# The last norm of a two-layer decoder trunk: weights applied early by ScalarE, the factor by VectorE and GpSimd

## What is computed

```python
def rmsnorm(x, g, eps=NORM_EPS):
    x32 = x.astype(jnp.float32)
    y = x32 * lax.rsqrt(jnp.mean(x32 * x32, axis=-1, keepdims=True) + eps)
    return (y * g.astype(jnp.float32)).astype(x.dtype)
...
        x = x + gt2 * conv_gated_mlp(h2, ffn_up[l], ffn_conv_w[l], ffn_conv_b[l], ffn_down[l])
    return rmsnorm(x, final_g)
```

## Time and profile before

| | us |
|---|---|
| median of three runs | 1070.72 |
| range of the three | 1070.26 to 1072.43 |
| the profiled execution, its own time | 1072.69 |
| its span, first to last instruction | 1070.9 |
| PE busy | 1048.0 (98%) |
| DVE busy | 849.9 (79%) |
| ACT busy | 587.2 (55%) |
| POOL busy | 115.6 (11%) |

### The profile page before, as it was taken

One profiled execution on the slowest core, in us unless ns is written; L12 is line 12 of the kernel. 1 busy time (PEld: TensorE's weight loads), 2 busy tenths in 40 slices (PEclk: granted clock), 3 DMA queues, 4 the chain that ended last, 5 costly groups with the idle time before them and its releaser, 6 DMA issues.

```text
span 1070.9 us, 24039 instructions
## 1 busy us (share of the span) xinstructions
PE 1048.0 (98%) x9982; PEld 961.1 (90%) x9982; DVE 849.9 (79%) x1272; ACT 587.2 (55%) x913; POOL 115.6 (11%) x138
## 2 busy tenths in 40 slices
PE   7999999999999999999999999999999999999997
PEld 6789988787789999999989999778877999999997
DVE  5698999686686898986779899968766788888763
ACT  2266567632465766663365575783328476666433
POOL 0100000055101000001120000002530100000001
PEclk9999999999999999999999999999999999999999
DMA  9955545544246766667865546451615565545651
GB/s 366 356 191 210 185 169 219 212 157 142 100 158 215 259 240 217 240 243 266 317 209 200 197 162 235 164 202 63 231 62 196 194 240 197 188 172 188 235 199 40
DMA packets 42088, 215.07 MB, mean 201 GB/s; under 512 B 8336, under 2 KB 8976, under 8 KB 22672
## 3 DMA queue, kind: packets, MB, share of 16 engines
q1 hardware_dynamic: 30480, 171.85, 43.9%
q0 software_dynamic: 11520, 41.95, 11.2%
HBM read 212.21 MB, written 1.05 MB: 199 GB/s over the span
## 4 chain that ended last, share of the span: by engine, by line
PE 83%; DVE 7%; DMA 7%; SPq 1%; ACT 1%; issue 1%; DVEq 0%; ACTq 0%
PE ps L1852 16%; PE ps L1853 16%; PE ps L1854 16%; PE ps L2066 6%; PE ps L2070 6%; PE ps L2064 6%; DMA mring<-wmod_dram 5%; PE ps L1872 4%; DVE macc L1144 2%; PE ps L2173 2%; DMA TK<-wmod_dram 2%; PE ps L1890 1%; PE ps L1816 1%; PE ps L2164 1%; PE ps L2021 1%
## 5 line engine op out<-in xcount | busy, mean ns | idle before, releaser
L995 ACT ACTIVATE WH<-ring 128x1024 fp32r<-128x1024 f32 x140 | 147.8, 1059 | 156.7 <-PE ps L1854 153.3
L1688 DVE TENSOR_TENSOR WLO<-ring,WH 128x1024 fp32r<-128x1024 f32 x140 | 169.2, 1222 | 58.0 <-ACT WH L995 57.9
L1853 PE MATMUL ps<-HL,WH 128*128 128x256 f32 x736 | 206.1, 280 | 0.0
L1854 PE MATMUL ps<-HH,WLO 128*128 128x256 f32 x736 | 206.1, 280 | 0.0
L1852 PE MATMUL ps<-HH,WH 128*128 128x256 f32 x736 | 205.0, 279 | 0.0
L1852 PEld LDWEIGHTS ps<-HH,WH 128*128 128x128 f32 x736 | 139.1, 189 | 0.1
L1853 PEld LDWEIGHTS ps<-HL,WH 128*128 128x128 f32 x736 | 137.6, 187 | 0.1
L1854 PEld LDWEIGHTS ps<-HH,WLO 128*128 128x128 f32 x736 | 137.6, 187 | 0.0
L578 POOL DMA_DIRECT2D mring<-wmod_dram x80 | 43.2, 540 | 751.3 <-DVE macc L1144 446.8
L1144 DVE SCALAR_TENSOR_TENSOR macc<-mring,sm,macc 128x1024 f32<-128x1024 f32 x70 | 96.5, 1378 | 17.0 <-DMA mring<-wmod_dram 14.7
L1852 PE MATMUL ps<-GH,WH 128*128 128x256 f32 x384 | 108.5, 282 | 0.4 <-DVE WLO L1688 0.4
(11 more groups left out here) (409 smaller groups left out, 2492.7 us busy)
## 6 DMA issues: line engine op xcount, KB each, us to landing
ring<-wmain_dram SPq DMA_DIRECT2D x150, 1024.0 KB, 5.0
mring<-wmod_dram POOLq DMA_DIRECT2D x80, 512.0 KB, 4.8
G<-wmod_dram SPq DMA_DIRECT2D x3, 1024.0 KB, 9.2
R<-wmod_dram SPq DMA_DIRECT2D x2, 1024.0 KB, 18.4
TK<-wmod_dram SPq DMA_DIRECT2D x2, 1024.0 KB, 20.0
X<-x_t_dram SPq DMA_DIRECT2D x1, 1024.0 KB, 5.1
R<-wmod_dram SPq DMA_DIRECT2D x2, 512.0 KB, 12.2
y_dram<-H SPq DMA_DIRECT2D x4, 256.0 KB, 2.2
```

What stands on the lines that cost most here:

```text
L995: A(WH[:, n % 2, part], ring[:, b, part], ACT.Copy).then_inc(hi_ready, 1)
L1688: V.tensor_tensor(WLO[:, n % 2, part], ring[:, b, part], WH[:, n % 2, part].bitcast(F32), ALU.subtract).then_inc(lo_ready, 1)
L1853: MM(out, w_high[:, at], low, start=False, stop=False, skip_group_check=True)
L1854: return MM(out, w_low[:, at], high, start=False, stop=stop, skip_group_check=True)
```

## The change

ScalarE: in `squares(4)`, behind each square, one more activation writes `X[m]` times the channel's final weight into `XB[m]`, and counts `gg_ready` (8 counts stand from the two layers, so 16 after the last). VectorE: in place of eight instructions with a weight and the factor, three plain products of `XB` and `RT`, of 2, 2 and 1 tiles, `RT` being repeated over the tiles (`over`). GpSimd: behind its last `add_squares`, one product of the same kind over tiles 5 to 7. SyncE: it still issues four transfers, of 2, 2, 1 and 3 tiles. The last waits for GpSimd (`sq_add` at 17) and stands behind the other three in the queue.

```diff
@@ -556,9 +556,11 @@
-            for j in range(4):
-                sp.wait_ge(h_pre, 8 * 4 + 2 * j + 2)
-                sp.dma_start(y_t[:, 2 * j:2 * j + 2, :], H[:, 2 * j:2 * j + 2, :]).then_inc(s_out, 16)
+            for j, (a, b) in enumerate(((0, 2), (2, 4), (4, 5))):
+                sp.wait_ge(h_pre, 8 * 4 + j + 1)
+                sp.dma_start(y_t[:, a:b, :], H[:, a:b, :]).then_inc(s_out, 16)
+            sp.wait_ge(sq_add, 17)
+            sp.dma_start(y_t[:, 5:8, :], H[:, 5:8, :]).then_inc(s_out, 16)
             sp.wait_ge(s_out, 64)
@@ -626,6 +628,9 @@
                 add_squares(2 * l + 2)
+            pool.wait_ge(gg_ready, 4 * L + KT)
+            pool.wait_ge(x_rt, 5)
+            pool.tensor_tensor(H[:, 5:8, :], XB[:, 5:8, 0:S], over(RT[:, :], 3), ALU.mult).then_inc(sq_add, 1)
@@ -659,6 +664,8 @@
                     A(H[:, m, :], X[:, m, :], ACT.Square).then_inc(x_sq, 1)
+                    if n == 4:
+                        A(XB[:, m, 0:S], X[:, m, :], ACT.Copy, scale=col(0, "fg", m)).then_inc(gg_ready, 1)
                 if b < KT:
                     return
@@ -1777,7 +1784,10 @@
                     residual(g1 + j, j, mod[:, u, :])
-            norm(4, col(0, "fg", 0, 8))
+            dve.wait_ge(gg_ready, 4 * L + KT)
+            dve.wait_ge(x_rt, 5)
+            for a, b in ((0, 2), (2, 4), (4, 5)):
+                V.tensor_tensor(H[:, a:b, :], XB[:, a:b, 0:S], over(RT[:, :], b - a), ALU.mult).then_inc(h_pre, 1)
```

## The result

The changed kernel takes 1073.61 us (median of nine runs, 1072.85 to 1077.69), the kernel before 1070.72 (median of nine, 1069.47 to 1072.43). The ratio is 1.0033, interval 1.0022 to 1.0045: slower by 0.33%, and by more than the 0.2% that counts as a difference here. The forecast was 1071.5, the range ended at 1072.7.

What follows compares the result with a forecast made beforehand. The prediction took the strict sequence from the last down projection to the output's landing as the bound. Products adding to 3.44 us and a larger last transfer gave 1070.72 + 0.75 = 1071.5 us, range 1069.6 to 1072.7.

Steps and rivals of the forecast that it cites:

- What bounds the kernel now: After the last down projection: one strict sequence to the output's landing; 6.0 us behind the factor, the change working on 3.25.
- the sum: Whole kernel: the last transfer lands 0.75 us later than now, so the median goes from 1070.72 to 1071.5 us.
- ScalarE's copies cost nothing: Final norm's squares: eight added copies delay nothing awaited, the last having 0.3 us of cover; 0, bounds 0 and +0.1 us.
- VectorE's part alone takes 1.62 us: Behind the factor: VectorE's three products over 5 tiles take 1.62 us, bounds 1.5 and 2.0, replacing 3.25 us.
- GpSimd's part alone takes 1.82 us: Behind the factor: GpSimd's one product of 768 elements takes 1.82 us undisturbed.
- They do not run in parallel, 3.44 us in all: Behind the factor: VectorE and GpSimd products, both with two SBUF inputs, block each other; 1.62 + 1.82 = 3.44 us against 3.25.
- GpSimd is first: Behind the factor: GpSimd runs 1065.02 to 1066.84, VectorE ends at 1068.32, last issue at 1068.68, landing at 1071.18 (+0.75 us).
- the third case in my list: Behind the factor: VectorE starts, GpSimd runs between its products, 1065.58 to 1067.40; last issue 1068.64, landing 1071.14 (+0.7 us).
- The rival of GpSimd at half speed for a repeated tile: GpSimd's product behind the factor takes 3.4 us or more, all added: 1073.1 us, slower by 2.4; chance 0.05.
- The range: Median time from 1069.6 us (both engines side by side, less 0.2) to 1072.7 us (+0.85 and 1.1 for scatter).
- the serial case: Behind the factor: VectorE's and GpSimd's products run one after the other; 0.45 to 0.85 us more than before, chance 0.76.
- What would show it: Profile signs: VectorE's first product about 2.4 us, both parts 3.3 to 3.5, output in one block starting 1.5 us later.

Runs made afterwards that it cites:

- the run with the early drain: Changed kernel with one more GpSimd drain, behind its last transfer and ahead of its last four adds of squares: 1071.78 us, ratio 1.0004 to the kernel before.
- the no-hold run: Changed kernel, but ScalarE also copies the factor to PSUM and VectorE reads it there: 1073.58 us, ratio 1.0035 to the kernel before.

## Why the prediction was wrong, point by point

- *What bounds the kernel now: the end is a strict sequence from the last down projection to the landing of the output.* Right for the kernel before. What I left out is that a second chain ran beside it and had only 4.3 us of cover: GpSimd's drain. I had read no row on line 199, though the trace of before shows it (7.39 us from 1058.8). This is the step that failed. The prediction took the 0.45 us from the last landing to the end of the span as fixed, as if nothing else could end it. In the part on GpSimd, the sum priced its product (1.82 us) and its transfer, and nothing that lies behind GpSimd's last instruction. The missing term is the drain: it sets the end at 2.28 + 6.62 + 0.23 = 9.13, which is 2.3 us behind the 6.80 at which the output would (9.13 - 6.79 by the run with the early drain). So of the 3.16 us more, the forecast had the kind and nearly the size of 0.82 and nothing of 2.34. That it said "later" at all is owed to the smaller part.
- *ScalarE's copies cost nothing.* Right. One pair took 0.73 us, and the last copy ended 0.40 us before the logarithm started (1060.32 + 0.49 to 1061.21), which came 1.21 us behind the start of the last square. It is 1.20 before (1062.80 to 1064.00); the 1.23 of the forecast is a slip.
- *VectorE's part alone takes 1.62 us.* Right: 1.62 with the factor in PSUM, and 2.50 for all eight tiles.
- *GpSimd's part alone takes 1.82 us.* Over-sized: 1.64 undisturbed, in the run with the factor in PSUM.
- *They do not run in parallel, 3.44 us in all.* Right in kind, and near in size: 3.07 us from VectorE's first start to its last end, with GpSimd inside.
- *GpSimd is first.* Wrong, but of small effect. VectorE was first, then GpSimd in between, then VectorE, the third case in my list, for which I gave the last issue at 3.71 behind the factor (1068.64) and the landing at 6.2. Measured: 3.72 and 6.39. The 384 KB took 2.67 us to land, not 2.50.
- *The rival of GpSimd at half speed for a repeated tile.* It gave 1073.1, near the measured 1073.6, by the wrong mechanism: the product was no slower than plain.
- *The range.* Its upper end was made of the serial case and scatter. With the drain as a case of its own (GpSimd's last end + 6.62 + 0.23 = 9.1 against 5.97) the sum would have been 1070.72 + 3.16 = 1073.9.
- *What would show it.* Several signs fail, and none of them points at the drain. VectorE's first product lasted 0.69 us and not 2.4 (the second was held, for 2.12), and both parts took 3.07 from first start to last end and not 3.3 to 3.5. The bytes moved in two blocks with about 1 us between them, and began no later behind the factor than before, where one block that starts 1.5 us later was forecast. The span moved by 2.8 us before 1062 us, in the lucky direction, and by 3.2 behind it.

The hold is the rule that I cited from the Trainium skill, SBUF — State Buffer, section "Who interferes with whom", and the no-hold run agrees with its condition too: with one SBUF input VectorE is free of GpSimd (1.62 us in place of 3.07).

## What to carry to other kernels

Before an instruction is moved to the end of a queue, read what the frame of the program does behind that queue's last instruction: here the answer on the frame's line, with the drain of each engine, and who it ends behind. If GpSimd issued many transfers of its own (80 here), let it do its last work early, or drain in an idle stretch first, which costs one line. The stretch must be long enough: the drain took 8.5 us of 24 here. Compare the tail from a common event and not the spans when single executions differ by more than the effect.

## What the runs showed of the hardware that I had not expected

- Behind a computing instruction, GpSimd's drain ends after 0.07 us plus about 82 ns for each transfer that GpSimd has issued since its last drain: 6.62 us for 80, 5.97 for 72, 0.73 for 8, 0.07 for none. An earlier drain takes the debt away. SyncE's drain takes 13 ns with 225 transfers. What GpSimd does in that time is not shown.
- In the view of waits, the time at the common end is put down to PE's queue (2.5 us), while the engine that came last was GpSimd. The drains of line 199 show it.
- GpSimd's product with a repeated second input takes 1.09 us for 512 elements and 1.64 for 768. Its additions of 512 take 1.274 and its product of two tiles of 512 without a repeat (L622 before) 1.31 to 1.33. So a repeated input does not slow it down. Whether it is what makes it faster was not tested apart, as the rows of 257 numbers are new too.
